# Expert products as plain fp32 matmuls on four 32-column tiles instead of split fp32r products

## The chip, the cores and the metric

The kernel runs on one core of a Trainium2 chip. The core's engines are TensorE (PE; its weight loads are recorded apart, as PEld), VectorE (DVE), ScalarE (ACT), GpSimd (POOL) and SyncE (SP), which only issues DMAs here. The metric is the device time of one execution in microseconds, as the median of several.

## What is computed

Two decoder layers over 256 tokens of width 1024, all in fp32. Layer 0 is sparse attention and a dense SwiGLU; then shared keys and values are projected; layer 1 is stick-breaking attention and a top-2-of-8 expert SwiGLU. The change is in the experts alone:

```python
D_MODEL, SEQ, D_FF, N_EXPERTS, TOP_K_EXPERTS = 1024, 256, 2816, 8, 2

def swiglu(u, w_gate_up, w_down):
    g, up = jnp.split(u @ w_gate_up, 2, axis=-1)
    return (jax.nn.silu(g) * up) @ w_down

def moe_ffn(u, router_w, w_gate_up, w_down):
    ...
    logits = (tok @ router_w).astype(jnp.float32)
    top_vals, top_idx = lax.top_k(logits, TOP_K_EXPERTS)
    gates = jax.nn.softmax(top_vals, axis=-1)
    ...
    for e in range(N_EXPERTS):
        y = y + dense_gates[:, e:e + 1].astype(tok.dtype) * swiglu(tok, w_gate_up[e], w_down[e])
```

An expert has 1024 x 5632 gate and up weights and 2816 x 1024 down weights, 4 bytes each: 34.6 MB, 277 MB for all eight.

## The kernel before

Every engine has its own instruction stream, written out by hand, and waits on semaphores; the order in the code is the order on the engine. No scheduler moves anything.

**Ahead of the experts** (to some 425 us) stand both attentions, the dense feed-forward and the routing. Some of their matmuls are plain fp32 (L531, L557, L578, L831, L898), the large ones are split as below. L578 (`index_scores`) has 64 contraction rows: its matmuls take partitions 0 to 63 and 64 to 127 in turn, so they sit on the upper and the lower half of the array. Its first run has 8 matmuls of 128 columns and 4 of 256, its second 4 of 256. L831 and L898 are loops over 8 blocks and 2 token halves, 16 matmuls each.

**Jobs.** A job is one expert for up to 96 tokens (`SLOTS`); with these inputs there are 8, and a Fori loop runs over the first seven, so it returns six times. The last job stands again behind an If. `gather` (L908) makes the transposed input of a job, 1024 x 96, from rows that GpSimd fetched; `slot_tokens` (L888) makes the row numbers.

**Tiles.** Gate and up weights come as 11 tiles (`STEPS`) of 1024 x 512: gate and up columns in turn, the last tile holding 256 of each. SP loads each in two DMAs of 1 MB into a ring of four slots (`up_ring`); the down weights come as 11 tiles of 256 x 1024, 1 MB each, into a ring of their own (`dn_ring`). Iteration i of a job has the first half (4 of 8 contraction blocks) of tile i (`expert_up`), the transposes of one group of hidden values (`hidden_T`), the second half, and the down tile i - 2 (`expert_dn`).

**Splitting.** A product in fp32 accuracy is made of three fp32r products (`product`, L500 to L502): hi x hi, hi x lo, lo x hi. For this ACT copies each half tile to fp32r (`up_half`, `dn_step`: L1031 in the profile), DVE subtracts that from the original (L1843, L1948), and PE reads the two copies. There are two copies of each, so the splits run up to two half tiles ahead of PE. The job's input and the hidden values are split too (`m_u_hi`, `m_u_lo`, `m_hT_hi`, `m_hT_lo`). SP may refill a ring slot when DVE has read it (`up_l`, `dn_l`).

**Hidden values.** The output of a gate or up tile is 96 x 512 in one PSUM bank. ACT takes SiLU of the gate (L1357), DVE multiplies with the up values (L1961), PE transposes the four blocks of 128 columns (L946), ACT and DVE copy them as hi and lo. The down products add up in one pair of banks over the job; then ACT and DVE copy the result out (`result`) and GpSimd writes it to `y_rows`. After the last job PE scatters its rows to tokens (L1000, L1003) and DVE adds them to `h`.

Of the kernel before, what the change touches and what calls it, by code (L numbers as in the profile page):

```python
# [17 lines left out]
P = 128  # L18
TOK = 256
NT = TOK // P  # L20
DM = 1024
# [43 lines left out]
def program(nc, x, a_norm_w, a_w_in, a_q_norm_w, a_k_norm_w, a_w_out, kv_norm_w, kv_w, b_norm_w,  # L65
# [6 lines left out]
    with ctx:  # L72
# [116 lines left out]
        m_hid = work[0:SLOTS, 0:1024].rearrange("p (b c) -> p b c", b=2)  # L189
# [7 lines left out]
        m_u_hi = uT_hi[:, :, :].rearrange("p k t -> p (k t)")[:, 0:KD * SLOTS]  # L197
        m_u_lo = uT_lo[:, :, :].rearrange("p k t -> p (k t)")[:, 0:KD * SLOTS]
        m_hT_hi = hid_hi[:, 0:4 * SLOTS].rearrange("p (f c) -> p f c", f=4)
        m_hT_lo = hid_lo[:, 0:4 * SLOTS].rearrange("p (f c) -> p f c", f=4)  # L200
# [49 lines left out]
        first_gather, first_u_h, first_u_l = sem("first_gather"), sem("first_u_h"), sem("first_u_l")  # L250

        e_silu, e_raw, e_hT, e_hT_h, e_hT_l = sem("e_silu"), sem("e_raw"), sem("e_hT"), sem("e_hT_h"), sem("e_hT_l")
        e_y_act, e_y_dve = sem("e_y_act"), sem("e_y_dve")
        e_pick, e_pickT, e_pickT_sb = sem("e_pick"), sem("e_pickT"), sem("e_pickT_sb")
        e_gather, e_u, e_u_h, e_u_l = sem("e_gather"), sem("e_u"), sem("e_u_h"), sem("e_u_l")
# [66 lines left out]
        def tile_cols(i):  # L322

            return 512 if i % STEPS < STEPS - 1 else FSTEP

        def hidden_blocks(g):

            return 4 if g % GROUPS < GROUPS - 1 else 2
# [35 lines left out]
        def _(sp):  # L364
# [112 lines left out]
        def _(pe):  # L477
# [445 lines left out]

            def expert_up(k, i, p):

                pe.wait_ge(up_l, job_piece(T_MOE, i, p + 1, k))
                if i == 0:
                    pe.wait_ge((first_u_l, e_u_l)[p], 1)
                elif i % STEPS == 0 and p == 0:
                    pe.wait_ge(e_u_l, k + (i // STEPS + 1))  # L930
                if i >= 3 and p == 0:
                    tile_free(k, i)
                hi, lo = (buffer(b, p, 2048).rearrange("p (k c) -> p k c", k=4) for b in (up_hi, up_lo))
                for j in range(4):
                    c = slice(SLOTS * (4 * p + j), SLOTS * (4 * p + j + 1))
                    mm = product(bank[tile_bank[i % STEPS % 3]][0:SLOTS, :], m_u_hi[:, c], m_u_lo[:, c],
                                 hi[:, j, :], lo[:, j, :], p == 0 and j == 0, p == 1 and j == 3)
                mm.then_inc(up_used, 1)

            def hidden_T(k, g):  # L940

                pe.wait_ge(e_raw, k * GROUPS + (g + 1))
                if g > 0:
                    pe.wait_ge(e_hT_l, k * GROUPS + g)
                for f in range(hidden_blocks(g)):
                    mm = pe.transpose(bank[6][:, SLOTS * f:SLOTS * f + SLOTS], m_hid[:, g % GROUPS % 2, P * f:P * f + P],  # L946
                                      ident[0:SLOTS, 0:SLOTS])
                mm.then_inc(e_hT, 1)

            def expert_dn(k, i):  # L950

                for f in range(2):
                    pe.wait_ge(dn_l, job_piece(STEPS, i, f + 1, k))
                    if f == 0:
                        pe.wait_ge(e_hT_l, k * GROUPS + (GROUPS * (i // STEPS) + i % STEPS // 2 + 1))
                    if i % STEPS == 0 and f == 0:
                        pe.wait_ge(e_y_act, k + (i // STEPS + 1))
                        pe.wait_ge(e_y_dve, k + (i // STEPS + 1))
                    block_f = 2 * (i % STEPS % 2) + f
                    for half in range(2):  # L960
                        c = slice(512 * half, 512 * half + 512)
                        mm = product(pair[1][0:SLOTS, c], m_hT_hi[:, block_f, :], m_hT_lo[:, block_f, :],
                                     buffer(dn_hi, f, DM)[:, c], buffer(dn_lo, f, DM)[:, c],
                                     i % STEPS == 0 and f == 0, i % STEPS == STEPS - 1 and f == 1)
                    mm.then_inc(dn_used, 1)
# [57 lines left out]
        def _(act):  # L1023
# [282 lines left out]
            def up_half(k, i, p):  # L1306
                if p == 0:
                    act.wait_ge(up_in[(T_MOE + i % STEPS) % RING], job_up_arrived(i % STEPS, k + i // STEPS))
                act.wait_ge(up_used, job_piece(T_MOE, i, p - 1, k))
                copy(buffer(up_hi, p, 2048), raw_piece(2 * (T_MOE + i % STEPS) + p)).then_inc(up_h, 1)  # L1310


# [4 lines left out]
            up_half(0, 0, 0)  # L1317
# [7 lines left out]
            up_half(0, 0, 1)  # L1325
            roots(3)
            for k in range(KD):
                if k % 2 == 0:
                    act.wait_ge(*((first_gather, k // 2 + 1) if k < KD - 2 else (e_gather, 1)))
                c = slice(SLOTS * k, SLOTS * k + SLOTS)  # L1330
                e = copy(m_u_hi[:, c], bank[gather_bank[k // 2]][:, SLOTS * (k % 2):SLOTS * (k % 2) + SLOTS],
                         nw[:, KD * NORM_F1 + k:KD * NORM_F1 + k + 1])
                if k % 2 == 1:
                    e.then_inc(first_u_h, 1)
# [6 lines left out]
            def gathered(k):  # L1341
# [3 lines left out]
                copy(m_u_hi, m_u).then_inc(e_u_h, 1)  # L1345

            def dn_step(k, i):
                for p in range(2):
                    if p == 0:
                        act.wait_ge(dn_in[(STEPS + i % STEPS) % RING], job_dn_arrived(i % STEPS, k + i // STEPS))  # L1350
                    act.wait_ge(dn_used, job_piece(STEPS, i, p - 1, k))
                    copy(buffer(dn_hi, p, DM), ffn_dn((STEPS + i % STEPS) % RING)[:, p, :]).then_inc(dn_h, 1)

            def silu_step(k, g):
                act.wait_ge(up_used, job_piece(T_MOE, STEPS * (g // GROUPS) + 2 * (g % GROUPS), 2, k))
                cols = tile_cols(STEPS * (g // GROUPS) + 2 * (g % GROUPS))
                act.activation(m_hid[:, g % GROUPS % 2, 0:cols], bank[tile_bank[2 * (g % GROUPS) % 3]][0:SLOTS, 0:cols],  # L1357
                               ACT.Silu).then_inc(e_silu, 1)

            def hidden_step(k, g):  # L1360
                act.wait_ge(e_hT, k * GROUPS + (g + 1))
                n = hidden_blocks(g)
                copy(m_hT_hi[:, 0:n, :], bank[6][:, 0:n * SLOTS].rearrange("p (f c) -> p f c", f=n)).then_inc(e_hT_h, 1)

            def result(k):
                act.wait_ge(dn_used, job_piece(STEPS, STEPS, 0, k))
                act.wait_ge(y_saved, k + 1)
                copy(m_y[:, 0:512], bank[2][0:SLOTS, :]).then_inc(e_y_act, 1)

            def iteration(k, i, last=False):  # L1370
                for p in range(2):
                    if i < STEPS or not last:
                        up_half(k, i, p)
                    if i == STEPS and p == 0 and not last:
                        gathered(k + 1)
# [5 lines left out]
                if i >= DN_LATE and (i - DN_LATE < STEPS or not last):  # L1381
                    dn_step(k, i - DN_LATE)
# [25 lines left out]
        def _(pool):  # L1408
# [93 lines left out]
            pool.wait_ge(up_l, job_piece(T_MOE, 7, 2, last_job))  # L1502
# [8 lines left out]
        def _(dve):  # L1511
# [329 lines left out]
            def up_half(k, i, p):  # L1841
                dve.wait_ge(up_h, job_piece(T_MOE, i, p + 1, k))
                dve.tensor_tensor(buffer(up_lo, p, 2048), raw_piece(2 * (T_MOE + i % STEPS) + p),  # L1843
                                  buffer(up_hi, p, 2048).bitcast(f32), ALU.subtract).then_inc(up_l, 1)

# [8 lines left out]
            up_half(0, 0, 0)  # L1854
# [48 lines left out]
            last.then_inc(e_pick, 1)  # L1903
            dve.wait_ge(total_ps, 1)
# [4 lines left out]
            for k in range(KD):  # L1909
                if k % 2 == 0:  # L1910
                    dve.wait_ge(first_u_h, k // 2 + 1)
                c = slice(SLOTS * k, SLOTS * k + SLOTS)
                last = dve.scalar_tensor_tensor(m_u_lo[:, c], bank[gather_bank[k // 2]][:, SLOTS * (k % 2):SLOTS * (k % 2) + SLOTS],
                                                nw[:, KD * NORM_F1 + k:KD * NORM_F1 + k + 1], m_u_hi[:, c].bitcast(f32),
                                                ALU.mult, ALU.subtract)
                if k % 4 == 3:
                    last.then_inc((first_u_l, e_u_l)[k // 4], 1)
            up_half(0, 0, 1)


# [159 lines left out]
```

## Time and profile before

| | |
|---|---|
| median of 3 runs | 1207.09 us (1205.64 to 1207.56) |
| the profiled execution's own time | 1206.92 us |
| its span on the core | 1205.2 us |
| PE busy | 1181.5 us, 98% of the span |
| weight loads busy | 898.9 us |
| DVE busy | 912.4 us |
| ACT busy | 776.4 us |
| moved by DMA | 359.81 MB, 299 GB/s over the span |
| granted PE clock | 0.998 of full |

Busy times of different engines overlap. Matmuls are pipelined: a record of a 512-column product lasts some 0.39 us, but the next begins 0.23 us after it, so the time between starts is the one that counts. Line numbers are those of the kernel before.

### The profile page before, as it was taken

The numbers are of one execution on the slowest core, as the hardware profiler recorded it, in microseconds if no ns is written. First come the engines' busy times: TensorE is split into PE (matmuls) and PEld (weight loads), VectorE is DVE, ScalarE is ACT, GpSimd is POOL, SyncE is SP. The second block draws the span as 40 slices with busy tenths as digits, with TensorE's granted clock in tenths as the row PEclk, the third lists the DMA queues.
The fourth block names the chain that finished last, engine by engine and source line by source line (L and its number), as shares of the span: only waits on it lengthen the run. The fifth ranks groups of instructions, "written<-read, shape, count | busy, mean of one in ns | idle before, by whom it ended". The sixth has DMA issues, their size and how long they took to land.

```text
span 1205.2 us, 16756 instructions
## 1 busy us (share of the span) xinstructions
PE 1181.5 (98%) x6064; PEld 898.9 (75%) x6064; DVE 912.4 (76%) x865; ACT 776.4 (64%) x792; POOL 61.0 (5%) x84
## 2 busy tenths in 40 slices
PE   8999999999999989999999999999999999999997
PEld 6768999998998757767767767777777776776674
DVE  3775654455643479898889898888888889888896
ACT  4765534433557467777777777777777768677773
POOL 0000000000000009000000000000000000000210
PEclk9999999999999999999999999999999999999999
DMA  9549964642452569999999999999999999999990
GB/s 333 202 132 291 362 211 163 237 140 70 140 202 78 209 218 395 317 381 395 352 371 396 348 373 394 366 356 396 379 341 395 392 329 397 393 342 342 396 369 36
DMA packets 174557, 359.81 MB, mean 299 GB/s; under 512 B 6632, under 2 KB 50064, under 8 KB 174512
## 3 DMA queue, kind: packets, MB, share of 16 engines
q1 hardware_dynamic: 170208, 343.78, 78.3%
q0 software_dynamic: 4080, 15.34, 3.8%
q8 instruction: 29, 0.48, 0.2%
q10 hardware_dynamic: 224, 0.09, 0.0%
q14 instruction: 16, 0.13, 0.0%
HBM read 347.65 MB, written 11.53 MB: 298 GB/s over the span
## 4 chain that ended last, share of the span: by engine, by line
PE 92%; DVE 4%; ACT 2%; DMA 1%; issue 1%; SPq 0%; ACTq 0%; DVEq 0%
PE pair L500 28%; PE pair L502 28%; PE pair L501 28%; PE pair L531 1%; PE pair L946 1%; DVE up_lo L1843 1%; ACT up_hi L1031 1%; PE pair L557 1%; DMA up_ring<-in_a_w_in 1%; PE pair L908 0%; DVE up_lo L1546 0%; PE pair L596 0%; DVE dn_ring L1650 0%; PE pair L898 0%; PE pair L831 0%
## 5 line engine op out<-in xcount | busy, mean ns | idle before, releaser
L1031 ACT ACTIVATE up_hi<-up_ring 128x2048 fp32r<-128x2048 f32 x222 | 424.9, 1915 | 214.9 <-PE pair L502 208.3
L1843 DVE TENSOR_TENSOR up_lo<-up_ring,up_hi 128x2048 fp32r<-128x2048 f32 x176 | 402.4, 2290 | 86.2 <-ACT up_hi L1031 83.7
L500 PE MATMUL pair<-up_hi,uT_hi 128*96 128x512 f32 (+1 forms) x832 | 332.2, 399 | 5.8 <-DVE up_lo L1843 4.4
L502 PE MATMUL pair<-up_hi,uT_lo 128*96 128x512 f32 (+1 forms) x832 | 327.6, 394 | 0.0
L501 PE MATMUL pair<-up_lo,uT_hi 128*96 128x512 f32 (+1 forms) x832 | 327.4, 393 | 0.0
L1948 DVE TENSOR_TENSOR dn_lo<-dn_ring,dn_hi 128x1024 fp32r<-128x1024 f32 x176 | 207.2, 1217 | 2.2 <-ACT dn_hi L1031 2.2
L1031 ACT ACTIVATE dn_hi<-dn_ring 128x1024 fp32r<-128x1024 f32 x198 | 201.4, 1050 | 8.5 <-PE pair L502 7.9
L1546 DVE TENSOR_TENSOR up_lo<-up_ring,up_hi 128x2048 fp32r<-128x2048 f32 x46 | 105.3, 2290 | 114.6 <-ACT up_hi L1031 114.6
L500 PEld LDWEIGHTS pair<-up_hi,uT_hi 128*96 128x96 f32 (+1 forms) x832 | 137.6, 165 | 62.5 <-DVE up_lo L1843 6.6
L502 PEld LDWEIGHTS pair<-up_hi,uT_lo 128*96 128x96 f32 (+1 forms) x832 | 137.7, 166 | 54.9
L501 PEld LDWEIGHTS pair<-up_lo,uT_hi 128*96 128x96 f32 (+1 forms) x832 | 137.9, 166 | 50.5
L500 PE MATMUL pair<-dn_hi,hid_hi 128*96 128x512 f32 (+1 forms) x432 | 171.4, 397 | 3.6 <-DVE hid_lo L1966 2.6
L501 PE MATMUL pair<-dn_lo,hid_hi 128*96 128x512 f32 (+1 forms) x432 | 170.4, 395 | 0.0
L502 PE MATMUL pair<-dn_hi,hid_lo 128*96 128x512 f32 (+1 forms) x432 | 170.3, 394 | 0.0
L500 PE MATMUL pair<-uT_hi,up_hi 128*128 128x256 f32 x480 | 135.6, 283 | 2.4 <-DVE uT_lo L1560 2.3
L501 PE MATMUL pair<-uT_lo,up_hi 128*128 128x256 f32 x480 | 134.9, 281 | 0.0
L502 PE MATMUL pair<-uT_hi,up_lo 128*128 128x256 f32 x480 | 134.9, 281 | 0.0
L500 PEld LDWEIGHTS pair<-dn_hi,hid_hi 128*96 128x96 f32 (+1 forms) x432 | 71.9, 166 | 31.3 <-DVE dn_lo L1948 4.5
L500 PEld LDWEIGHTS pair<-uT_hi,up_hi 128*128 128x128 f32 x480 | 90.5, 189 | 3.7 <-issue 2.9
L502 PEld LDWEIGHTS pair<-dn_hi,hid_lo 128*96 128x96 f32 (+1 forms) x432 | 71.9, 166 | 28.5
L501 PEld LDWEIGHTS pair<-dn_lo,hid_hi 128*96 128x96 f32 (+1 forms) x432 | 71.9, 166 | 26.8
L501 PEld LDWEIGHTS pair<-uT_lo,up_hi 128*128 128x128 f32 x480 | 90.5, 189 | 0.4
(295 smaller groups left out, 842.2 us busy)
## 6 DMA issues: line engine op xcount, KB each, us to landing
up_ring<-in_moe_w_gate_up SPq DMA_DIRECT2D x176, 1024.0 KB, 11.1
dn_ring<-in_moe_w_down SPq DMA_DIRECT2D x88, 1024.0 KB, 13.5
up_ring<-in_dense_w_gate_up SPq DMA_DIRECT2D x22, 1024.0 KB, 9.1
dn_ring<-in_dense_w_down SPq DMA_DIRECT2D x11, 1024.0 KB, 11.0
up_ring<-in_kv_w SPq DMA_DIRECT2D x4, 2048.0 KB, 8.1
y_rows<-q_T POOLq DMA_DIRECT2D x1, 6528.0 KB, 33.5
up_ring<-in_a_w_in SPq DMA_DIRECT2D x4, 1024.0 KB, 12.8
up_ring<-in_a_w_out SPq DMA_DIRECT2D x2, 2048.0 KB, 9.4
```

The lines of the kernel that those rows point to most:

```text
L500: pe.matmul(ps, a_hi, b_hi, start=start, stop=False, skip_group_check=shared)
L501: pe.matmul(ps, a_hi, b_lo, start=False, stop=False, skip_group_check=shared)
L502: return pe.matmul(ps, a_lo, b_hi, start=False, stop=stop, skip_group_check=shared)
L531: mm = pe.matmul(bank[2 * t + g][:, 0:I_HALF], uT_in[:, k, P * t:P * t + P], index_tile(half)[:, j, I_HALF * g:I_HALF * g + I_HALF], start ...
L557: mm = pe.matmul(bank[(NT * j + t) % 4][:, 0:cols], uT_in[:, k, P * t:P * t + P], up_tile(j, cols)[:, k, :], start=(k == 0), stop=(k == KD ...
L946: mm = pe.transpose(bank[6][:, SLOTS * f:SLOTS * f + SLOTS], m_hid[:, g % GROUPS % 2, P * f:P * f + P], ident[0:SLOTS, 0:SLOTS])
L1031: return act.activation(out_, in_, ACT.Copy, scale=scale)
L1546: dve.tensor_tensor(buffer(up_lo, n, 2048), raw_piece(n), buffer(up_hi, n, 2048).bitcast(f32), ALU.subtract).then_inc(up_l, 1 + unsplit)
L1843: dve.tensor_tensor(buffer(up_lo, p, 2048), raw_piece(2 * (T_MOE + i % STEPS) + p), buffer(up_hi, p, 2048).bitcast(f32), ALU.subtract).the ...
L1948: dve.tensor_tensor(buffer(dn_lo, p, DM), ffn_dn((STEPS + i % STEPS) % RING)[:, p, :], buffer(dn_hi, p, DM).bitcast(f32), ALU.subtract).th ...
```

## The change

- The expert products are plain fp32 matmuls on operands as they were loaded. The split copies of expert weights, of a job's input and of the hidden values are gone from ACT and DVE, with their semaphores. `m_u_now` and `m_hT` take the place of the hi and lo buffers. The dense layers are split as before.
- Each matmul takes 32 of the 96 slots as its stationary columns (`THIRD`) and a place 0 to 3 in the array (`tile_position=(0, 32 * place)`), with the 32 PSUM partitions that belong to it. Of a gate or up tile, places 0 to 2 make the first 384 columns of their third of the slots; place 3 makes the last 128 columns of all three thirds, one after another. So a bank holds the tile as 128 x 384 and not as 96 x 512. The down product is divided likewise: places 0 to 2 make columns 0 to 767, place 3 makes 768 to 1023 for the three thirds.
- SiLU, multiply and transposes run over 128 x 384 (three blocks of 128 instead of four of 96 rows). The last group has half the columns and takes two instructions where the others take one, and three for its copy. The result is copied out in five pieces instead of two.
- SP waits for PE's use of a ring slot (`up_used`, `dn_used`), and PE waits for the arrival of a load itself.
- The first job's input is scaled by ACT and DVE in turn, two of eight blocks at a time.

```diff
-        m_hid = work[0:SLOTS, 0:1024].rearrange("p (b c) -> p b c", b=2)
+        m_hid = work[:, 0:768].rearrange("p (b c) -> p b c", b=2)
...
-                        sp.wait_ge(up_l, job_free(T_MOE, i % STEPS, k + i // STEPS))
+                        sp.wait_ge(up_used, job_free(T_MOE, i % STEPS, k + i // STEPS))
...
-                        sp.wait_ge(dn_l, job_free(STEPS, m % STEPS, k + m // STEPS))
+                        sp.wait_ge(dn_used, job_free(STEPS, m % STEPS, k + m // STEPS))
...
+            def on_third(out, a, w, place, start, stop):
+                return pe.matmul(out, a, w, start=start, stop=stop, tile_position=(0, THIRD * place), skip_group_check=True)
...
             def expert_up(k, i, p):
-                pe.wait_ge(up_l, job_piece(T_MOE, i, p + 1, k))
+                s = (T_MOE + i % STEPS) % RING
+                if p == 0:
+                    pe.wait_ge(up_in[s], job_up_arrived(i % STEPS, k + i // STEPS))
...
-                hi, lo = (buffer(b, p, 2048).rearrange("p (k c) -> p k c", k=4) for b in (up_hi, up_lo))
-                for j in range(4):
-                    c = slice(SLOTS * (4 * p + j), SLOTS * (4 * p + j + 1))
-                    mm = product(bank[tile_bank[i % STEPS % 3]][0:SLOTS, :], m_u_hi[:, c], m_u_lo[:, c],
-                                 hi[:, j, :], lo[:, j, :], p == 0 and j == 0, p == 1 and j == 3)
+                ps = bank[tile_bank[i % STEPS % 3]]
+                for j in range(4 * p, 4 * p + 4):
+                    start, stop = j == 0, j == KD - 1
+                    thirds = [m_u_now[:, SLOTS * j + THIRD * n:SLOTS * j + THIRD * n + THIRD] for n in range(3)]
+                    if whole_tile(i):
+                        w = up_tile(T_MOE + i % STEPS)[:, j, :]
+                        for n in range(3):
+                            on_third(part_of(ps, n)[:, 0:384], thirds[n], w[:, 0:384], n, start, stop)
+                        for n in range(3):
+                            mm = on_third(part_of(ps, 3)[:, P * n:P * n + P], thirds[n], w[:, 384:512], 3, start and n == 0, stop)
...
             def expert_dn(k, i):
...
+                    for n in range(3):
+                        on_third(part_of(y, n)[:, 0:512], thirds[n], w[:, 0:512], n, start, stop)
+                    for n in range(2):
+                        on_third(part_of(y, 3)[:, 256 * n:256 * n + 256], thirds[n], w[:, 768:1024], 3, start and n == 0, stop)
+                    for n in range(3):
+                        on_third(part_of(y, n)[:, 512:768], thirds[n], w[:, 512:768], n, start, stop)
+                    on_third(part_of(y, 3)[:, 512:768], thirds[2], w[:, 768:1024], 3, start, stop).then_inc(dn_used, 1)
...
             def result(k):
                 act.wait_ge(dn_used, job_piece(STEPS, STEPS, 0, k))
                 act.wait_ge(y_saved, k + 1)
-                copy(m_y[:, 0:512], bank[2][0:SLOTS, :]).then_inc(e_y_act, 1)
+                copy(m_y[:, 0:512], bank[2][0:SLOTS, :])
+                copy(m_y[0:32, 768:1024], bank[2][96:128, 0:256])
+                copy(m_y[32:64, 768:1024], bank[2][96:128, 256:512]).then_inc(e_y_act, 1)
```

PE before, about the transposes of a group (L946) between two halves of a gate or up tile:

```order
L500 MATMUL pair<-up_hi,uT_hi 96x512
L501 MATMUL pair<-up_lo,uT_hi 96x512
L502 MATMUL pair<-up_hi,uT_lo 96x512
L946 MATMUL pair<-cst,work 128x96 x4
L500 MATMUL pair<-up_hi,uT_hi 96x512
L501 MATMUL pair<-up_lo,uT_hi 96x512
L502 MATMUL pair<-up_hi,uT_lo 96x512
```

PE after, at the same place (L970 are the transposes):

```order
L926 MATMUL pair<-up_ring,work 32x384 x3
L926 MATMUL pair<-up_ring,work 32x128 x3
L970 MATMUL pair<-cst,work 128x128 x3
L926 MATMUL pair<-up_ring,work 32x384 x3
L926 MATMUL pair<-up_ring,work 32x128 x3
```

Three instructions per step have become six (three for the places 0 to 2, three for place 3), and they read the ring and no copy. The transposes stand where they stood.

PE before, between the two 128-row blocks of a down tile:

```order
L500 MATMUL pair<-dn_hi,hid_hi 96x512
L501 MATMUL pair<-dn_lo,hid_hi 96x512
L502 MATMUL pair<-dn_hi,hid_lo 96x512
L953 REGISTER_ALU
L500 MATMUL pair<-dn_hi,hid_hi 96x512
L501 MATMUL pair<-dn_lo,hid_hi 96x512
L502 MATMUL pair<-dn_hi,hid_lo 96x512
```

PE after, the last step of a gate or up tile and the down tile behind it:

```order
L926 MATMUL pair<-up_ring,work 32x384 x3
L926 MATMUL pair<-up_ring,work 32x128 x3
L926 MATMUL pair<-dn_ring,kT_a 32x512 x3
L926 MATMUL pair<-dn_ring,kT_a 32x256 x6
L926 MATMUL pair<-dn_ring,kT_a 32x512 x3
```

A block of a down tile was six instructions of 512 columns and is now nine, three of 512 and six of 256.

ACT before, in one iteration of a job (`hid_hi` is the copy of the transposed values):

```order
L1031 ACTIVATE up_hi<-up_ring 128x2048
L1309 REGISTER_ALU
L1031 ACTIVATE up_hi<-up_ring 128x2048
L1351 REGISTER_ALU
L1031 ACTIVATE dn_hi<-dn_ring 128x1024
L1351 REGISTER_ALU
L1031 ACTIVATE dn_hi<-dn_ring 128x1024
L1361 ISA
L1031 ACTIVATE hid_hi<-pair 128x384
```

ACT after, in two iterations:

```order
L1375 ACTIVATE work<-pair 128x384
L1382 REGISTER_ALU
L1064 ACTIVATE kT_a<-pair 128x384
L1372 REGISTER_ALU
L1375 ACTIVATE work<-pair 128x384
```

Of ACT's work in a job the four copies of each iteration are gone; SiLU and the copy of the transposed values follow each other directly.

## Rows read from the trace of the kernel before

**Rows 1.** The chain of work that ended last, in order of time: start us, us, what.

```profile
448.13 0.33 PE pair L946 x4
...
577.30 0.33 PE pair L946 x4
...
672.11 0.33 PE pair L946 x4
...
1180.60 0.33 PE pair L946 x4
```

**Rows 2.** Stretches: busy us (records) of PE, PEld, DVE, ACT, POOL; clock, DMA share, GB/s.

```profile
577.30:672.11 94.81, 94.77 (x433) 66.54 (x431) 83.60 (x63) 69.70 (x59) 2.10 (x4) 1.00 1.02 374
448.00:465.00 17.00, 17.00 (x78) 11.91 (x77) 15.67 (x12) 12.45 (x11) 12.70 (x12) 1.00 1.04 401
```

**Rows 3.** Waits of 577.3 to 672.1: who waited for whom: us in total, times, longest.

```profile
ACT up_hi L1031 <- PE pair L502: 13.2, 15, 1.7
DVE up_lo L1843 <- ACT up_hi L1031: 10.7, 12, 1.2
```

**Rows 4.** Timeline of PE, two starts a step apart: start us, us, line, shapes.

```profile
561.50 0.39 PE L500 MATMUL pair<-up_hi,uT_hi 128*96 128x512 f32 x1
...
562.19 0.40 PE L500 MATMUL pair<-up_hi,uT_hi 128*96 128x512 f32 x1
```

**Rows 5.** PE groups by shape: count | busy us, mean ns | idle before, releaser.

```profile
L500 PE MATMUL pair<-up_hi,uT_hi 128*96 128x512 f32 x704 | 280.5, 398 | 4.7 <-DVE up_lo L1843 4.4
...
L500 PE MATMUL pair<-dn_hi,hid_hi 128*96 128x512 f32 x352 | 139.8, 397 | 3.6 <-DVE hid_lo L1966 2.6 <-DVE dn_lo L1948 1.0
```

**Rows 6.** The chain again, plain fp32 products and transposes ahead of the experts.

```profile
70.54 5.15 PE pair L557 x12
...
115.30 0.87 PE pair L488 x8
...
417.92 2.73 PE pair L831 x24
...
425.50 3.83 PE pair L898 x32
```

**Rows 7.** L578 alone, stretch by stretch: PE busy us (matmuls), weight loads (loads).

```profile
42.08:42.40 0.32, 0.31 (x2) 0.30 (x4) 1.00 0.00 0
42.40:42.62 0.22, 0.22 (x4) 0.19 (x2) 1.00 0.00 0
42.84:43.10 0.26, 0.26 (x4) 0.00 (x0) 1.00 0.00 0
```

**Rows 8.** Timeline of PE about the first L578.

```profile
36.82 0.39 PE L502 MATMUL pair<-up_hi,uT_lo 128*128 128x512 f32 x1
37.14 2.03 PE L578 MATMUL pair<-dn_ring 64*128 64x128 f32 x24
39.09 0.50 PE L500 MATMUL pair<-up_hi,uT_hi 128*128 128x512 f32 x1
```

**Rows 9.** Waits of PE from 429 to 448.2.

```profile
PE pair L500 <- DVE up_lo L1843: 4.0, 4, 2.0
```

**Rows 10.** Timeline of PE near the end, with the idle time before and its releaser.

```profile
1187.52 0.47 PE L500 MATMUL pair<-dn_hi,hid_hi 128*96 128x512 f32 x1 [1.03 <-DVE dn_lo L1948]
...
1193.30 0.44 PE L500 MATMUL pair<-dn_hi,hid_hi 128*96 128x512 f32 x1 [2.60 <-DVE hid_lo L1966]
```

**Rows 11.** Records before 546 us; instruction queues before it, and from 546 to 1102.

```profile
0.00:546.00 546.00, 531.81 (x3133) 444.77 (x3134) 338.24 (x439) 304.91 (x391) 37.40 (x53) 1.00 0.65 228
...
q8 instruction: 25, 0.41, 0.3%
...
q14 instruction: 2, 0.02, 0.0%
```

**Rows 12.** DMA issues: count, KB each, median us from issue to landing.

```profile
y_rows<-q_T POOLq DMA_DIRECT2D x7, 384.0 KB, 6.6
...
out<-h SPq DMA_DIRECT2D x4, 256.0 KB, 2.4
```

More of the change, by code:

```diff
@@ L196, in program @@
         m_u = q_flat[:, DM:DM + KD * SLOTS]
[L197 to L200, printed above, removed]
+        m_u_now = work[:, 768:768 + KD * SLOTS]
+        m_hT = kT_a[:, :, :].rearrange("p h t -> p (h t)")[:, 0:3 * P].rearrange("p (f c) -> p f c", f=3)
         y_first = u
@@ L320, in program, with whole_tile, whole_group @@
         DN_LATE = 2
[L322 to L328, printed above, removed]
+        THIRD = SLOTS // 3
+        def whole_tile(i):
+            return i % STEPS < STEPS - 1
+        def whole_group(g):
+            return g % GROUPS < GROUPS - 1
         def silu_group(i):
@@ L943, in hidden_T @@
                 if g > 0:
[L944 to L947, printed above, removed]
+                    pe.wait_ge(e_hT_h, k * GROUPS + g)
+                for f in range(3):
+                    mm = pe.transpose(bank[6][:, P * f:P * f + P], m_hid[:, g % GROUPS % 2, P * f:P * f + P], ident)
@@ L948, in hidden_T, with hidden_third @@
                 mm.then_inc(e_hT, 1)
-            def expert_dn(k, i):
-                for f in range(2):
[L953 to L965, printed above, removed]
+            def hidden_third(i, f, n):
+                block = 2 * (i % STEPS % 2) + f
+                if block < 3:
+                    return m_hT[:, block, THIRD * n:THIRD * n + THIRD]
+                return m_hT[:, n, SLOTS:SLOTS + THIRD]
@@ L1304, in _ @@
             up_piece(2 * T_BO + 3)
[L1306 to L1310, printed above, removed]
             def stream_T(half):
@@ L1324, in _ @@
             squares_half(3, 1)
-            up_half(0, 0, 1)
             roots(3)
[L1327 to L1334, printed above, removed]
+            for b, known in ((0, first_u_act), (2, e_u_now)):
+                act.wait_ge(first_gather, b + 1)
+                for k in (2 * b, 2 * b + 1):
+                    c = slice(SLOTS * k, SLOTS * k + SLOTS)
+                    e = copy(m_u_now[:, c], bank[gather_bank[b]][:, SLOTS * (k % 2):SLOTS * (k % 2) + SLOTS],
+                             nw[:, KD * NORM_F1 + k:KD * NORM_F1 + k + 1])
+                e.then_inc(known, 1)
             act.wait_ge(route_top, 1)
@@ L1344, in gathered @@
                 act.wait_ge(up_used, job_piece(T_MOE, 0, 0, k))
[L1345 to L1352, printed above, removed]
@@ L1354, in silu_step @@
-            def silu_step(k, g):
[L1355 to L1358, printed above, removed]
+                copy(m_u_now, m_u).then_inc(e_u_now, 1)
+            def silu_step(k, g):
+                tile = STEPS * (g // GROUPS) + 2 * (g % GROUPS)
+                act.wait_ge(up_used, job_piece(T_MOE, tile, 2, k))
+                gate, v = bank[tile_bank[2 * (g % GROUPS) % 3]], m_hid[:, g % GROUPS % 2, :]
+                if whole_group(g):
+                    act.activation(v, gate[:, 0:384], ACT.Silu).then_inc(e_silu, 1)
+                else:
+                    act.activation(v[0:SLOTS, 0:192], gate[0:SLOTS, 0:192], ACT.Silu)
+                    act.activation(v[SLOTS:P, :].rearrange("p (n c) -> p n c", n=3)[:, :, 64:128],
+                                   gate[SLOTS:P, 0:192].rearrange("p (n c) -> p n c", n=3), ACT.Silu).then_inc(e_silu, 1)
@@ L1367, in result @@
                 act.wait_ge(y_saved, k + 1)
-                copy(m_y[:, 0:512], bank[2][0:SLOTS, :]).then_inc(e_y_act, 1)
+                copy(m_y[:, 0:512], bank[2][0:SLOTS, :])
+                copy(m_y[0:32, 768:1024], bank[2][96:128, 0:256])
+                copy(m_y[32:64, 768:1024], bank[2][96:128, 256:512]).then_inc(e_y_act, 1)
             def iteration(k, i, last=False):
[L1371 to L1375, printed above, removed]
+                if i == STEPS and not last:
+                    gathered(k + 1)
                 if i == STEPS + 2:
@@ L1908, in _ @@
             last.then_inc(route_top, 1)
[L1909 to L1918, printed above, removed]
+            first_slots(3)
             def gathered(k):
                 dve.wait_ge(e_gather, k + 1)
+                dve.wait_ge(e_u_now, k)
                 w = nw[:, KD * NORM_F1:KD * (NORM_F1 + 1)].rearrange("p (b j) -> p b j", b=2).unsqueeze(3)\
@@ L1986, in iteration @@
                     result(k)
-                if i >= DN_LATE and (i - DN_LATE < STEPS or not last):
-                    dn_step(k, i - DN_LATE)
-                if g is not None and (g < GROUPS or not last):
-                    hidden_lo(k, g)
                 if i == 4 and not last:
```

98 lines of the change are left out of this document (53 added, 45 removed).

## The prediction

> **What bounds the kernel now.** I looked first at the chain of work that ended last: TensorE (PE) is on it for 92% of the span. Its repeating rows give the period. The transposes of one job stand at 577.30 us and again at 672.11, so a job takes 94.8 us, and the stretch that repeats, from 448.13 to 1180.60, is 732.5 us or 7.73 jobs [rows 1]. In one period PE is busy for 94.77 of 94.81 us, with a granted clock of 1.00, with DVE at 83.6 and ACT at 69.7 [rows 2]. The waits of that period are those of ACT and DVE for each other and for PE [rows 3]; PE waits for nobody. So the split copies that the change removes (DVE's and ACT's 83.6 and 69.7 us) are hidden work. They give nothing by themselves. The result hangs on what PE needs for the same products in the new form, and after that on what the short stretches at both ends of the expert stage lose to the copies today.
>
> **PE's products, now.** One step (one block of 128 rows of a gate or up tile) is three fp32r products of 512 columns; it takes 0.69 us, from 561.50 to 562.19 [rows 4]. There are 704 such steps and 352 for the down weights [rows 5], in eight jobs: 88 and 44 each, the latter two to a 128-row block, 22 blocks.
>
> **PE's products, changed.** First the price of a plain fp32 product. The trace has L898 with 32 records where the program has 16 matmuls: a plain product is two records, each with a weight load of its own. A record of 512 columns takes 5.15/12 = 0.429 us (L557). For 128 columns there are the transposes of L488, 0.87/8 = 0.109 us, and L831's matmul records, 2.73/24 = 0.114 with a gap ahead of one; I take 0.109 [rows 6]. One of 256 takes 0.216 us where a row shows it (42.40 to 42.62) [rows 7]. 384 columns lie half way between 256 and 512: 0.3225 us, an estimate. On one array these products would cost 2 x 0.429 = 0.858 us in place of 0.69, so all hangs on the four column tiles running at once. The trace has no column tiles, but it has their nearest kin, L578, whose matmuls alternate between rows 0 to 63 and rows 64 to 127. There each window of 0.22 us holds two records that run and two that begin [rows 7], and 24 records (16 of 128 columns, 8 of 256) need 16 x 0.109 + 8 x 0.216 = 3.5 us in a row but stand in 2.03 [rows 8]. Halves of the array do work in parallel, with plain fp32, at the full rate of each. I take the same for four column tiles.
>
> By that, in a gate or up step tiles 0 to 2 have two records of 384 columns each (0.645 us) and tile 3 has six of 128 (0.654 us): the step takes 0.654. In a down block tile 3 has six records of 256 (1.296 us), the others 2 x 0.429 + 2 x 0.216 = 1.290: 1.296. A job is 88 x 0.654 + 22 x 1.296 = 57.6 + 28.5 = 86.1 us, against 88 x 0.69 + 22 x 1.38 = 91.1 now.
>
> The transposes of the hidden values are 18 of 128 x 128 (0.109 each: 2.0 us) in place of 22 at 0.33/4 [rows 1]; the eight of the gather and the small slot products stay at about 1.0. New are the changes between four tiles and the whole array: six groups of transposes, a gather and the slot product make eight round trips per job. L578's excursion shows what one costs: the array is free at 36.82 + 0.23 = 37.05, the next ordinary product stands at 39.09, so 2.04 us for work of 16/2 x 0.109 + 8/2 x 0.216 = 1.74: 0.30 us, and some 0.1 more before the product after it follows [rows 8]. 8 x 0.41 = 3.3 us. The job comes to 86.1 + 2.0 + 1.0 + 3.3 = **92.4 us**, 2.4 less than now. Over 7.73 jobs that is **-18.6 us**. Bounds: a round trip that costs nothing makes it -44; records stretched by 2.8% make it nothing.
>
> **First tiles.** Today PE waits four times, 4.0 us, for the split of the first tiles [rows 9]. These waits go: the tiles landed before and are read where they lie. In their place PE waits for the scaled gather (m_u_now), which ACT and DVE now share; its last quarter is copied under the first four steps. The 20 steps up to 448.13 shrink by 20 x 0.036 = 0.7. **-4.6 us**, bounds -2 and -6.
>
> **Last tiles.** PE idles 1.03 and 2.60 us for the last down splits [rows 10]. The first goes; of the second the copy of the last transposes stays, now three small copies behind one another, about 1.1 us. The last three down tiles give 0.1 to 0.2 each. At the very end ACT has two more copies of 32 rows before the scatter can begin, about 0.8 us on the path. 3.6 - 1.1 + 0.5 - 0.8 = **-2.2 us**, bounds 0 and -4.
>
> **Waits that are moved.** SP now frees a ring slot after PE has used it, not after DVE has split it, about half a tile (3 us) later, but a tile is also needed later by the same, since no split goes ahead of PE. Nobody waited for an expert load [rows 3]. A job's bytes are 374 GB/s x 94.8 us = 35.5 MB; the queues have moved 401 GB/s over 17 us [rows 2], so loads alone would need 88.4 us a job. That doesn't reach 92.4, and it limits a job that were faster: no gain over 6.4 x 7.73 = 49 us. ACT's copy of the next job's input (128 x 768) must follow the last gate-up tile; it lies beside a down tile of 2 x 1.296 us. SiLU and multiply now have two idle engines.
>
> **The loop.** A matmul now carries four records with its weight loads, and the job has 726 in place of 396 products: about 2,960 records against 864 (433 + 431) [rows 2]. What the program occupies can be read off the instruction queue: 25 packets, 0.41 MB, for the 6,267 records before 546 us, about 65 bytes each; and from 546 to 1102 us, six rounds of the loop, that queue has no packet at all [rows 11]. Today's loop body, some 56 KB, stays on the chip. The new one is some 190 KB. Whether that stays no row can say. If not, each of six returns has to wait for its first packet. The shortest transfers of the trace land after 2.4 us, those beside the expert loads after 6.6 [rows 12]; some 0.9 us of queued records go off beforehand. The ends are 0 and 6 x 6.6 = 40 us. I take 2.2 each, near the short end since a packet is small (16 KB): **+13 us**, because a body 3.4 times as large is further from what the trace shows to be held than from what it shows to be fetched.
>
> The Trainium skill, "Runtime: NRT & Kernel Launch", Instruction fetch mechanics, gives PE 128 KiB of instruction memory and says that a taken branch out of the window it holds stalls for the fetch of its target. By that the returns do stall; it gives no time for one, and with the body held the sum would be 13 us lower.
>
> **The sum**, against the profiled execution: span 1205.2 - 18.6 - 4.6 - 2.2 + 13 = 1192.8; 1.9 us lie between its span and the median of the three runs: **1194.7 us**. Own range of this case 1186 to 1204: 10 us below for cheaper round trips, 9 above for dearer returns.
>
> **The rivals.**
> 1. The loop stays on the chip or its return is hidden: 1194.7 - 13 = 1182, down to 1165 with cheap changes of tiling. For it: nothing in rows 11 shows a fetch in the loop. Against: the body's size.
> 2. Instructions become a cost of their own: returns at 6.6 us each (+27, 1222), or packets late in the run of the body, one each 8 us instead of 22 before. A step has 24 records in 0.654 us, 27 ns each; L578's 48 came at 2.03/48 = 42 ns, limited by its own length. From 28.8 ns a record PE is no faster than today. 1205 to 1240.
> 3. The queue starts records strictly in order. Both records of a product belong to one tile, so the second holds up the tiles behind it: a step is 3 x 0.3225 + 5 x 0.109 = 1.51 us, a down block 2.80, a job 201, the kernel 1207 + 106 x 7.73 - 7 = 2020 us. Against it stand rows 7: with strict order the eight records of 42.09 would begin and end with one alone, 5 intervals, and they stand in four.
> 4. Four tiles can't all be fed. Each streams its own columns over all 128 partitions: 4 x 384/0.3225 = 4.8 columns per ns against 512/0.23 = 2.2 now. L578 says nothing on this, since its two halves read different partitions. Two at a time make the products 172 us a job and the kernel 1207 + 84 x 7.73 - 7 = 1850. It decides from a stretch of 2.8% on.
>
> The Trainium skill, "TensorE: Matmul & The Clock Gate", What overlaps and what doesn't, calls matmuls strictly first in, first out in start and end. That is rival 3, and rows 7 speak against it as a rule for tiles: the result by it would be 2020 us instead of 1195.
>
> **How the numbers follow.** A measurement of this kernel tells 0.2% (2.4 us) from no change. Forecast (about 1195) 0.42; rival 1 0.18; rival 2 0.20, of which 0.06 fall within 0.2%; rival 3 0.08; rival 4 0.12. The range 1165 to 1240 takes the first three, 0.80. Faster 0.42 + 0.18 less a hundredth: 0.59; same 0.07; slower 0.14 + 0.08 + 0.12 = 0.34.
>
> **What would show it.** Right: a period near 92.4 us between the gathers, steps of 0.65 us with four records at once, weight loads hidden, round trips of 0.4 us, DVE and ACT idle for most of the stage, an instruction queue with 11 or 12 packets per job and a gap of 2 us on PE at each return. Wrong: steps of 1.5 (rival 3) or 1.3 us (rival 4), a PE that waits for a load, a job near 89 us with loads behind (the queues bound), or no gap at the returns.

## The result and the profile after

The changed kernel takes **1215.66 us** (median, 1214.33 to 1217.66), the kernel before beside it 1206.74: a ratio of 1.0073, interval 1.006 to 1.0086. It is slower, by 0.7%, where 1% faster was forecast. The profiled execution has a span of 1213.8 us, 8.6 more than before. Its page: the busy times, the instruction queue, the chain's shares, and the largest group of PE (L926 is the line of `on_third`, which every expert product goes through).

```profile
PE 1168.2 (96%) x14480; PEld 1017.5 (84%) x14480; DVE 288.6 (24%) x470; ACT 284.3 (23%) x476; POOL 30.5 (3%) x84
...
q8 instruction: 130, 2.13, 0.7%
...
PE 91%; issue 3%; DVE 3%; ACT 1%; DMA 1%; SPq 0%; ACTq 0%; DVEq 0%
...
L926 PE MATMUL pair<-up_ring,work 128*32 128x128 f32 (+1 forms) x8448 | 507.0, 386 | 30.2 <-issue 30.2
```

PE was busy for 98% of the span and is for 96%; DVE fell from 912.4 to 288.6 us of work and ACT from 776.4 to 284.3, and neither gave anything, as expected of hidden work. New is "issue": time in which PE waits for nothing that the profile shows, 30.2 us of it ahead of L926. It lies in one kind of place. The chain of waits about the second of them:

```profile
632.37 5.35 PE pair L926 x48
637.72 4.65 issue
642.37 5.11 PE pair L926 x30
647.48 0.33 issue
647.81 2.26 PE pair L926 x19
```

From 637.72 PE stands still for 4.65 us. Six such places stand 98.7 to 98.8 us apart (538.96, 637.72, 736.39, 835.15, 933.97, 1032.79), 4.65 to 4.74 us long, and each is the place where the Fori loop goes back. Three stretches of the trace, in the columns of [rows 2]: a whole period, the 3.4 us behind its return, and the 3.4 us after those.

```profile
637.72:736.39 98.67, 93.69 (x1482) 81.46 (x1482) 5.71 (x13) 8.34 (x20) 1.85 (x4) 0.98 0.99 361
642.37:645.77 3.40, 3.40 (x34) 3.04 (x38) 0.00 (x0) 0.00 (x0) 0.00 (x0) 0.51 1.05 405
645.77:649.17 3.40, 3.07 (x58) 2.47 (x51) 0.00 (x0) 0.00 (x0) 0.00 (x0) 0.99 1.03 383
```

The period is 98.67 us against 94.81 before [rows 2]. Behind the return the granted clock is at its lower level (0.51 of full, 1.2 GHz) for 3.4 us (4.2 behind the last return). PE has 34 records at work in them where the next 3.4 us have 58; and those next 3.4 us hold a second, small gap, the 0.33 us of 647.48 in the chain.

Away from the returns the new form runs as worked out. The first expert tiles, from the chain:

```profile
428.56 13.24 PE pair L926 x120
441.80 0.48 PE pair L970 x3
442.27 15.80 PE pair L926 x144
458.07 0.48 PE pair L970 x3
```

Between two groups of transposes (441.80 and 458.07) lie 16 steps and 4 down blocks: 16 x 0.654 + 4 x 1.296 = 15.65 us by the prediction, and 15.80 are there, which hold the way back from the transposes too.

### The profile page after: what moved, and what is told of

Read it like the earlier page. It is cut to its first block, busy times and chain, and to the rows that moved or that the text cites. A ratio compares the mean times of both kernels' runs of the same rounds, so it can differ in the third digit from the quotient of the medians.

```text
span 1213.8 us, 31928 instructions
## 1 busy us (share of the span) xinstructions
PE 1168.2 (96%) x14480; PEld 1017.5 (84%) x14480; DVE 288.6 (24%) x470; ACT 284.3 (23%) x476; POOL 30.5 (3%) x84
## 4 chain that ended last, share of the span: by engine, by line
PE 91%; issue 3%; DVE 3%; ACT 1%; DMA 1%; SPq 0%; ACTq 0%; DVEq 0%
PE pair L926 59%; PE pair L500 8%; PE pair L501 8%; PE pair L502 8%; PE pair L970 2%; PE pair L531 1%; PE pair L557 1%; DMA up_ring<-in_a_w_in 1%; DVE up_lo L1569 1%; DVE dn_ring L1664 1%; PE pair L908 0%; ACT up_hi L1064 0%; PE pair L596 0%; DVE dn_ring L1673 0%; PE pair L898 0%
## 5 line engine op out<-in xcount | busy, mean ns | idle before, releaser
L926 PE MATMUL pair<-up_ring,work 128*32 128x128 f32 (+1 forms) x8448 | 507.0, 386 | 30.2 <-issue 30.2
L926 PEld LDWEIGHTS pair<-up_ring,work 128*32 128x32 f32 x8448 | 477.3, 111 | 53.7 <-issue 44.4
L926 PE MATMUL pair<-dn_ring,kT_a 128*32 128x256 f32 (+1 forms) x3168 | 250.8, 451 | 0.8 <-ACT kT_a L1064 0.8
L926 PEld LDWEIGHTS pair<-dn_ring,kT_a 128*32 128x32 f32 x3168 | 160.0, 110 | 60.0 <-issue 1.2
L1569 DVE TENSOR_TENSOR up_lo<-up_ring,up_hi 128x2048 fp32r<-128x2048 f32 x46 | 105.3, 2291 | 114.0 <-ACT up_hi L1064 113.9
L1064 ACT ACTIVATE up_hi<-up_ring 128x2048 fp32r<-128x2048 f32 x46 | 87.9, 1913 | 104.4 <-PE pair L502 98.5
L502 PEld LDWEIGHTS pair<-uT_hi,up_lo 128*128 128x128 f32 x480 | 90.4, 188 | 0.0
L500 PE MATMUL pair<-up_hi,uT_hi 128*128 128x512 f32 x128 | 51.7, 404 | 1.1 <-DVE uT_lo L1592 1.1
L501 PE MATMUL pair<-up_lo,uT_hi 128*128 128x512 f32 x128 | 50.5, 395 | 0.0
L502 PE MATMUL pair<-up_hi,uT_lo 128*128 128x512 f32 x128 | 50.5, 395 | 0.0
## 6 DMA issues: line engine op xcount, KB each, us to landing
dn_ring<-in_dense_w_down SPq DMA_DIRECT2D x11, 1024.0 KB, 11.4
```

Source lines behind the costliest of these rows:

```text
L500: pe.matmul(ps, a_hi, b_hi, start=start, stop=False, skip_group_check=shared)
L501: pe.matmul(ps, a_hi, b_lo, start=False, stop=False, skip_group_check=shared)
L502: return pe.matmul(ps, a_lo, b_hi, start=False, stop=stop, skip_group_check=shared)
L926: return pe.matmul(out, a, w, start=start, stop=stop, tile_position=(0, THIRD * place), skip_group_check=True)
L1064: return act.activation(out_, in_, ACT.Copy, scale=scale)
L1569: dve.tensor_tensor(buffer(up_lo, n, 2048), raw_piece(n), buffer(up_hi, n, 2048).bitcast(f32), ALU.subtract).then_inc(up_l, 1 + unsplit)
```

## The experiments

The theory after the result: the products are as fast as forecast, and what eats the gain is the return of a loop body that is too large to be held on the chip. Rivals: the late time lies in the tiles themselves (the changes of tiling, or records stretched now and then), or it is the mere amount of instructions, jump or no jump.

**No return.** Only the Fori loop goes; the same instructions run.

```diff
-            with pe.Fori(0, NEXP - 1) as k:
-                job(k)
+            for k in range(NEXP - 1):
+                job(k)
```

> The changed kernel with PE's loop over the first seven jobs written out seven times, so PE never jumps back; nothing else differs. Theory A (the loss is the six returns of PE's loop: an idle gap of 5.07 us each, of which 0.3 belongs to the last records, then 3.4 us at half clock, together some 6.5 us a return): no gap over 1 us on PE between the jobs, granted clock near 1.00 throughout, a job of 92.2 to 92.4 us, and 1215.7 - 39 = 1177 us. Theory B (the loss is spread over the products, the changes between four tiles and the whole array, or waits): 1213 to 1218 us and jobs of 98 us. A third outcome: the loads become the bound, jobs of 93 to 94 us with PE waiting for a load, 1185 to 1190 us.

Measured: 1173.61 us, ratio to the kernel before 0.9728 (0.9714 to 0.9743); 3.4 us below the expected 1177, since a return costs more than the 6.5 expected. One job, and the waits of PE from 450 to 1180 us:

```profile
583.65:674.99 91.34, 91.34 (x1487) 80.33 (x1483) 5.71 (x13) 8.33 (x20) 1.86 (x4) 1.00 1.04 387
```

```profile
PE pair L926 <- DMA up_ring<-in_moe_w_gate_up: 2.8, 3, 1.9
PE pair L1033 <- ACT q_T L1064: 1.6, 1, 1.6
PE pair L926 <- ACT kT_a L1064: 0.8, 1, 0.8
```

A job takes 91.34 us, at full clock from end to end, and no wait of PE for "issue" is left. So a return costs 98.76 - 91.34 = 7.4 us and six cost 44.5: near 5.0 that PE stands still (the start of the record behind is 5.03 to 5.12 us after the one ahead), 1.7 for 3.4 us at half clock, and the rest by the end of the second gap. The two traces hold the same 14,480 records of PE in the same order, so the delay can also be counted record by record: behind a return PE is 4.9 to 5.0 us late at its first record, 6.5 to 7.0 when the clock is back, and 7.3 to 7.5 from 12 us behind the gap on. The kernel gains 42.1 of the 44.5 us, as PE now waits 2.8 us for loads. The amount of instructions alone costs nothing: their queue moves 71 packets from 546 to 1102 us (79 in the changed kernel with its loop), and no two neighbouring starts of PE's records are more than 1 us apart there. Out of the six returns comes the whole loss, and more: without them the new form beats the kernel before by 2.7%.

**No return in the kernel before.** The same edit there.

> The kernel before with PE's loop over the first seven jobs written out, the control of the first run. Theory A (a return costs only when the body, here some 56 KB, is not held on the chip): within 0.2% of 1207 us, jobs of 94.8 us, instruction packets all along the expert stage. Theory B (writing out a loop helps any kernel, by another way): faster by several us.

Measured: 1207.97 us, ratio 1.0007 (0.9997 to 1.0017); jobs of 94.8 us. Its loop returned for free, so the unrolled form wins nothing by itself. Its instruction queue from 546 to 1102 us shows the size of a job, 20 packets of 16 KB for 5.9 jobs, 56 KB each:

```profile
q8 instruction: 20, 0.33, 0.2%
```

**How large a body is held.** The kernel before with a loop body of three jobs (two rounds, one return; some 168 KB), and of two (`Fori(0, 3)` and `range(2)`; three rounds, two returns; some 112 KB), the rest written out:

```diff
-            with pe.Fori(0, NEXP - 1) as k:
-                job(k)
+            with pe.Fori(0, 2) as r:
+                for part in range(3):
+                    job(r * 3 + part)
+            job(6)
```

> The kernel before with three jobs in the body of PE's loop (about 168 KB of records, 2 rounds, then the seventh job written out): one return, from job 3 to job 4. Theory A: one gap of 4 to 5 us on PE there with half clock after it, and a time of 1207 + 6 = 1213 us. Theory B (the gap belongs to the tiled products or to the smaller time that queued records cover, 27 ns each in place of 115): no gap, 1207 us; a gap shorter than 5 us by the longer cover of slower records would be in between, about 2 us.

> The kernel before with two jobs in the body of PE's loop (about 112 KB of records, 3 rounds, two returns). Theory A with a limit above this size: no gap and 1207 us. If what is held is less than 112 KB: two gaps, 1219 us. Theory B: no gap.

Measured: 1212.74 us for the body of three and 1218.5 for that of two, one execution each; the kernel before had a median of 1207.11 beside them. PE in the timeline of the body of three jobs, then of two jobs (the start, us, and the idle time ahead):

```profile
740.84 0.74 PE L500 MATMUL pair<-up_hi,uT_hi 128*96 128x512 f32 x1 [3.27 <-issue]
```

```profile
645.90 0.73 PE L500 MATMUL pair<-up_hi,uT_hi 128*96 128x512 f32 x1 [3.30 <-issue]
```

Both bodies stall at each return, and nowhere else between the jobs: starts 3.5 to 3.7 us apart (737.18 to 740.84; 642.21 to 645.90 and 838.01 to 841.53), then the lower clock; the job with the return takes 99.8 us (body of three), 101.0 and 99.7 us (body of two), against 94.8. That is 5.0 us of the 5.6 that the first kernel lost, and 11.1 of the 11.4 of the second. The products are the old ones, so the gap does not belong to tiles or plain fp32. A body of 56 KB is held and one of 112 KB is not. The gap is shorter than in the changed kernel. One possible reason is that there a record starts each 27 ns and here each 115 ns (three records in 0.69 us with their weight loads), so that the same number of records waiting on PE's side would cover more of the wait. The instruction queue shows another difference: a single packet is fetched in each of these gaps, and two about each gap of the changed kernel, 1.4 to 2.7 us apart. In all eleven stalled returns (the run with two jobs per round, below, taken in) PE's next record starts 2.7 to 3.1 us after the start of the last packet in the gap. So the longer gap goes with a second packet; that this is the cause was not tested, and neither was the first reason.

**Two jobs per round in the changed kernel.** Two returns of a body of some 380 KB.

```diff
-            with pe.Fori(0, NEXP - 1) as k:
-                job(k)
+            with pe.Fori(0, 3) as r:
+                for part in range(2):
+                    job(r * 2 + part)
+            job(NEXP - 2)
```

> The changed kernel with a loop of three rounds over two jobs each, and the seventh job written out: the same instructions are executed, but there are two returns of a body twice as large instead of six, and one more stretch of straight code. Theory (a return costs 7.4 us wherever it goes back farther than what is held, and straight code is fetched without a stall): two returns, 1173.6 + 2 x 7.4 = 1188.4 us, gaps of 5.1 us on PE at two places, every other job at 91.3 us. Rival (it is the amount of code fetched, and not the jump, that costs: 2 x as much per return): gaps near 10 us or jobs above 91.3 us without a return in them, 1200 us or more. Prediction's value of 2.2 us a return: 1178 us.

Measured: 1186.90 us, ratio 0.9834 (0.9819 to 0.9849). The two places in the timeline of PE:

```profile
633.39 5.45 PE L926 MATMUL pair<-up_ring,work 128*32 128x384 f32 x57 [4.89 <-issue]
...
823.87 2.78 PE L926 MATMUL pair<-up_ring,work 128*32 128x384 f32 x22 [4.90 <-issue]
```

The jobs with a return take 99.1 and 99.0 us, all others 91.34; the records stand 5.27 and 5.28 us apart at the gaps. The cost goes with the number of returns (7.7 us each, 0.3 more than with the small body: the gap is 0.2 us longer, and the low clock lasts 4.1 and 4.8 us behind it), hardly with the size of the body. That is the theory's 1188.4 within 2 us, and neither rival's number.

**What the four tiles give.** The changed kernel with its plain products on the whole array, 96 x 512, loop kept.

```diff
-                for j in range(4 * p, 4 * p + 4):
-                    ...
-                            on_third(part_of(ps, n)[:, 0:384], thirds[n], w[:, 0:384], n, start, stop)
+                for j in range(4):
+                    c = slice(SLOTS * (4 * p + j), SLOTS * (4 * p + j + 1))
+                    mm = pe.matmul(ps, m_u_now[:, c], w[:, j, :], start=(p == 0 and j == 0), stop=(p == 1 and j == 3))
```

> The changed kernel with its plain fp32 products on the whole array (96 slots by 512 columns, no column tiles), the loop kept. Theory (the four tiles give what the step gained; a body that the chip holds returns without a gap): a plain product costs two records of 0.429 us, so a gate or up step 0.858 us, a down block 1.716, a job 88 x 0.858 + 22 x 1.716 + 2.8 = 116 us, no gap at the six returns (the body has some 1,000 records with its weight loads, as small as that of the kernel before), and the kernel 1207 + (116 - 94.8) x 7.73 - 7 = about 1364 us. Rival (the gap at the returns belongs to the form of the change, waits on the loads' semaphores or plain products, and not to the size of the body): the same step and job, but a gap of some 5 us at each return, about 1400 us. A third: two records of one plain product share something on the whole array and a step is under 0.8 us, under 1330 us.

Measured: 1368.66 us, ratio 1.1333 (1.131 to 1.1356). One job, and three rows of the chain (a down tile, a half tile, the transposes):

```profile
512.72:628.86 116.14, 116.14 (x299) 45.71 (x298) 5.90 (x11) 7.54 (x15) 1.90 (x4) 1.00 0.84 305
```

```profile
639.99 3.43 PE pair L980 x8
643.42 3.43 PE pair L948 x8
646.86 0.33 PE pair L957 x4
```

A half tile of four steps and a down tile of two blocks both take 3.43 us, which is 8 x 0.429; the job is 116.14 us where 116 was worked out. No gap stands at the returns and the clock is 1.00: plain products and waits on the loads' semaphores don't make one. The body is small (299 records and 298 weight loads a job, not the 1,000 expected), which fits the theory. The four tiles take 24.8 us off a job (116.14 to 91.34), and PE without them would have made the change 13% slower.

**What a change of tiling costs.** On the unrolled kernel, the transposes of a group in two places, which adds six changes per job.

```diff
-                for f in range(3):
+                for f in blocks:
                     mm = pe.transpose(bank[6][:, P * f:P * f + P], m_hid[:, g % GROUPS % 2, P * f:P * f + P], ident)
...
+                    if j == 2 and g is not None:
+                        hidden_T(k, g, range(1))
```

> The changed kernel unrolled, with the transposes of a group in two places: one of the three after the second of the four steps of the first half tile, the other two where all three stood. Same work, six more changes of tiling per job. Theory (0.27 us for each): + 6 x 0.27 x 7.73 = 12.5 us, 1186 us, jobs of 93.0 us. By the 0.41 us of the prediction: + 19 us, 1192.6 us. Rival (changes of tiling cost nothing and the gap is a wait): no change, 1172 to 1175 us.

Measured: 1183.01 us, ratio 0.9794 (0.9777 to 0.981). The chain about one group:

```profile
694.22 0.26 PE pair L972
694.48 1.45 PE pair L926 x12
695.92 0.37 PE pair L972 x2
```

The jobs take 93.06 us, 1.72 more: 0.29 us for each change to the whole array and back, and the 0.26 us in which a single transposition of 0.109 stands in the chain shows half of it. The whole kernel pays 9.4 us, less than 7.73 x 1.72 = 13.3: the unrolled kernel waited 2.8 us for loads, this one never. The last 1.1 us are not traced to anything.

**Two changes fewer.** On the unrolled kernel again, the slot product and the gather moved beside a group's transposes.

```diff
+                if i == 8 and not last:
+                    gather(k + 1)
+                if i == 6 and not last:
+                    pe.wait_ge(e_u, k + 1)
+                    slot_tokens(k + 1)
                 if up:
                     expert_up(k, i, 1)
...
-                if i == 8 and not last:
-                    gather(k + 1)
-                if i == 5 and not last:
-                    pe.wait_ge(e_u, k + 1)
-                    slot_tokens(k + 1)
```

> The changed kernel unrolled, with the small slot product and the gather of a job moved beside the transposes of a group that stand in the same iteration: the same work, two changes of tiling fewer in each of seven jobs. Theory (each costs 0.29 us, as the run with split transposes shows it: jobs of 93.06 against 91.33 us): jobs of 90.75 us and 0.58 x 7 = 4 us less than 1173.6: 1169.6 us. Rival (the loads set the end by now: the unrolled kernel's last jobs waited 2.8 us in all for gate and up tiles, the run with split transposes not at all): the jobs are as short, but the last two wait for loads by what is gained, and the time stays at 1172 to 1175 us.

Measured: 1172.34 us, ratio 0.9718 (0.9705 to 0.9732), not to be told from the unrolled kernel's 0.9728. Waits of PE from 440 to 1185 us, and two stretches:

```profile
PE pair L926 <- DMA up_ring<-in_moe_w_gate_up: 5.4, 5, 1.8
```

```profile
600.00:700.00 100.00, 100.00 (x1640) 89.10 (x1636) 6.51 (x15) 10.18 (x24) 1.87 (x4) 1.00 1.04 387
...
1000.00:1100.00 100.00, 98.30 (x1594) 86.08 (x1585) 5.45 (x11) 9.44 (x22) 3.99 (x7) 1.00 1.04 385
```

The jobs are shorter as the theory had it, 90.74 us for four of them, and then 91.04 and 92.79: PE waits 5.4 us for gate and up tiles. The rival holds. The queues move 385 to 387 GB/s, the 35.4 MB of a job take 35.4 / 386 = 91.7 us, and the ring's lead is used up after five jobs. From here on a faster PE brings nothing.

## Why the prediction was wrong

The time lies inside the range (1165 to 1240) and on the other side of the kernel before. The profiled spans, stretch by stretch (first transposes at 447.96 and 441.73 us, the last but one at 1180.44 and 1191.31):

| stretch | before | after | difference | forecast |
|---|---|---|---|---|
| ahead of the first expert product | 429.10 | 428.49 | -0.6 | 0 |
| first tiles, to the first transposes | 18.86 | 13.24 | -5.6 | -4.6 |
| 7.73 jobs, without returns | 732.5 | 705.1 | -27.4 | -18.6 |
| six returns | 0 | 44.5 | +44.5 | +13 |
| from the last but one transposes on | 24.77 | 22.47 | -2.3 | -2.2 |
| span | 1205.2 | 1213.8 | +8.6 | -12.4 |

The 705.1 is the stretch's 749.6 less 6 x 7.42.

- **What bounds the kernel:** right. DVE and ACT lost two thirds of their work and the time follows PE alone.
- **PE's products, changed:** right to the third digit. The step was 0.654 and the down block 1.296 us by estimate; a whole job with its changes of tiling fits them (2.24 us are left for the eight changes, where the split transposes' 0.29 each make 2.3), and the whole-array run fits the 0.858 of the other form. Inside a step the records of places 0 to 2 start 6 to 7 ns apart and those of place 3 each 109 ns. Rival 3 (strict order) and rival 4 (tiles can't all be fed) are out; four tiles stream 4 x 384 columns in 0.3225 us.
- **Changes of tiling:** right in kind, too dear in size. 0.41 us each were taken from L578's excursion [rows 8], 0.28 is what a job leaves (91.34 - 86.1 - 3.0 = 2.24 us for eight) and 0.29 what the split transposes add. 8 x 0.13 x 7.73 = 8 us of the job term are this. L578 goes between halves of the rows and the whole array, not between column tiles; which part of its 0.41 us was the change no run shows.
- **First tiles, last tiles:** right within 1.0 and 0.1 us. At the end PE stands idle for 1.1 us at the last transposes, as forecast, and the scatter waits for two more copies of ACT:

```profile
1199.72 0.55 PE L970 MATMUL pair<-cst,work 128*128 128x128 f32 x3
1201.09 2.80 PE L926 MATMUL pair<-dn_ring,kT_a 128*32 128x512 f32 x36 [0.82 <-ACT kT_a L1064]
1205.53 1.96 PE L1033 MATMUL pair<-q_T,work 96*128 96x512 f32 x4 [1.64 <-ACT q_T L1064]
```

- **The loop** is the step that failed: "I take 2.2 each, near the short end since a packet is small". That the body is not held was right, and so was the count of packets for the straight form (11 or 12 a job forecast; 71 in 6.1 jobs, 11.7 each); with the returns it is 79 in 5.6 rounds, 14 each. But the term priced a return as one short transfer less queued records. It has three parts: the standstill of 5.0 us, 3.4 us at half clock behind it (1.7 us), and what is lost from there to the end of a second gap, some 0.7 us. The second part was nowhere in the sum, although the granted clock is in every row of the profile; the third neither. In the gap not one but two instruction packets of 16 KB are fetched (in that of 637.34 to 642.37 us their records begin 0.2 and 2.3 us into it, each 1.1 us long), and PE goes on 2.7 to 2.8 us after the second began. So a landing of 2.4 us [rows 12] is near the time behind one packet, and what the standstill has beyond it goes with the second; the 6.6 us landing beside the expert loads is longer than the whole standstill. Rival 2 had dear returns as its first half, with 1222 us for 6.6 each; measured are 7.4 and 1216. That these lie close is partly luck: the returns were dearer than it took, and the jobs shorter.
- **Waits that are moved:** right for the forecast itself, PE waits for no load. The bound was wrong: 401 GB/s held over 17 us [rows 2], not over a job. 386 is what lasts, 91.7 us a job in place of 88.4. The loads would have capped any better outcome at some 1170 us, as the run with two changes fewer shows (1172.34).

The Trainium skill, "Runtime: NRT & Kernel Launch", Instruction fetch mechanics, says that a taken branch out of the window that is held stalls for the fetch of its target, and that straight code is streamed with its cost mostly hidden. Both agree with the runs here: 5.0 us of gap at a return, none in the unrolled kernel. The 128 KiB that it gives PE are not a size up to which a loop returns for free: a body of 112 KB stalled.

What stays open: between 56 and 112 KB, where the limit lies; what the second gap behind a return is (a packet's record runs from 645.4 to 646.4 us ahead of the gap of 647.5, but that PE waits for it is not shown; in the kernel before with large bodies, counted record by record against its unrolled form, less than 0.1 us is lost once the clock is back); why the first of the two fetched packets does not release PE; and what a return would cost beside idle queues, since every return here stands beside full ones. Transposes on the four tiles, which would save seven of the eight changes, were not measured; with the loads as the next bound, little of it could be expected to show.

## What to carry to other kernels

When a change multiplies the instructions of a loop body, price the return by itself: the gap, and the low clock after it, times the number of rounds; and look at whether unrolling, which costs nothing where the code streams, takes it away. One landing taken from the trace doesn't price such a gap: here one or two packets were fetched in it, and PE went on 2.7 to 3.1 us after the last of them began. And before spending on a faster engine, work out the next bound from a rate that holds over a whole period.

## What the runs showed of the hardware

- Plain fp32 on four 32-column tiles runs all four at their full rate, 12 records in 0.654 us; a step costs 5% less than three fp32r products on the whole array (0.69) and 24% less than plain fp32 on it (0.858). A change between the tiles and the whole array and back costs 0.29 us.
- Straight code is supplied for 32.5 records and weight loads per us (1,487 + 1,483 in 91.34) from 430 to 1100 us without a gap beyond 1 us; the instruction queue carries 16 KB each 7.8 us for it.
- A return of a body that isn't held costs 7.3 to 7.8 us at 27 ns a record and 4.9 to 6.2 us at 115 ns, of which the low clock is between a fifth and a half. A body of 56 KB returns for free, one of 112 KB stalls.
- The gap at a return of the changed kernel hardly depends on the size of the body: 5.03 to 5.12 us at 190 KB, 5.27 and 5.28 at 380 KB.
- A 16 KB instruction packet's record is as long beside idle queues as beside full ones: in the trace before, 1.23 us at 353 us, where the queues move 5 GB/s, and 1.14 us at 488, where they move 357.
